# A decoder trunk on one core: VectorE waits for a GpSimd copy, and a group of weight loads waits for a transposed tile

## The reference

```python
for l in range(DEPTH):      # DEPTH = 2
    x = x + HALF_STEP * swiglu(rmsnorm(x, norm_ffn1[l]), w1_gate[l], w1_up[l], w1_down[l])
    ...                     # h = rmsnorm(x); differential attention and retention from h @ w_in
    x = x + mixed @ w_out[l]
    x = x + HALF_STEP * swiglu(rmsnorm(x, norm_ffn2[l]), w2_gate[l], w2_up[l], w2_down[l])
return rmsnorm(x, norm_final)
```

## Time and profile before

| | us |
|---|---|
| median of 3 runs | 958.66 (958.51 to 961.71) |
| profiled execution | 959.83 |
| its span in the trace | 957.9 |
| TensorE matmul busy | 945.5 (99% of the span) |
| VectorE busy | 556.7 (58%) |
| ScalarE busy | 460.5 (48%) |
| GpSimd busy | 189.2 (20%) |
| granted TensorE clock | 0.998 of full speed |

### The profile page before, as it was taken

How to read it: one execution, slowest core, us unless ns; L and a number is a source line. 1 busy time by engine, 2 the same in 40 slices (tenths; PEclk the granted TensorE clock), 3 DMA queues, 4 the chain that set the end, 5 groups by cost and what they waited for, 6 DMA issues and landing times.

```text
span 957.9 us, 12612 instructions
## 1 busy us (share of the span) xinstructions
PE 945.5 (99%) x4369; PEld 782.9 (82%) x4369; DVE 556.7 (58%) x632; ACT 460.5 (48%) x592; POOL 189.2 (20%) x239
## 2 busy tenths in 40 slices
PE   8999999999999999999999999999999999999997
PEld 6888888888888888888888888888888887888885
DVE  5545555666666565555656555556665756555554
ACT  7534444465563454444445444444657445444442
POOL 4344321000011322121033111110002024211110
PEclk9999999999999999999999999999999999999999
DMA  8897776634363886675647766663724657866641
GB/s 269 238 223 221 237 232 194 225 133 153 111 215 102 233 242 230 196 229 193 225 141 203 231 194 230 197 230 132 242 74 168 220 127 206 260 196 223 192 157 44
DMA packets 166339, 185.98 MB, mean 194 GB/s; under 512 B 49296, under 2 KB 139456, under 8 KB 166304
## 3 DMA queue, kind: packets, MB, share of 16 engines
q1 hardware_dynamic: 122368, 174.09, 54.2%
q10 hardware_dynamic: 43616, 10.52, 6.8%
q0 software_dynamic: 320, 0.92, 0.7%
HBM read 173.96 MB, written 1.05 MB: 183 GB/s over the span
## 4 chain that ended last, share of the span: by engine, by line
PE 93%; DMA 2%; ACT 2%; DVE 1%; POOL 1%; issue 0%; SPq 0%; POOLq 0%; DVEq 0%; ACTq 0%
PE gu L920 20%; PE gu L922 19%; PE gu L921 19%; PE acc L920 10%; PE acc L922 10%; PE acc L921 10%; DMA kT<-kT 2%; PE tp L1119 1%; DVE w_lo L628 1%; PE tp L938 1%; ACT w_hi L377 1%; PE acc L1130 1%; PE tp L1142 1%; DMA x<-in_x_dram 1%; PE gu L946 0%
## 5 line engine op out<-in xcount | busy, mean ns | idle before, releaser
L628 DVE TENSOR_TENSOR w_lo<-raw,w_hi 128x2048 fp32r<-128x2048 f32 (+1 forms) x164 | 375.1, 2292 | 153.1 <-ACT w_hi L377 152.7
L920 PE MATMUL gu<-w_hi,xT_hi 128*128 128x512 f32 x862 | 338.3, 392 | 0.2 <-DVE w_lo L628 0.2
L922 PE MATMUL gu<-w_hi,xT_lo 128*128 128x512 f32 x862 | 335.9, 390 | 0.0
L921 PE MATMUL gu<-w_lo,xT_hi 128*128 128x512 f32 x862 | 335.7, 389 | 0.0
L377 ACT ACTIVATE w_hi<-raw 128x2048 fp32r<-128x2048 f32 (+1 forms) x164 | 305.6, 1867 | 13.4 <-DMA raw<-in_w_in_dram 7.1
L920 PEld LDWEIGHTS gu<-w_hi,xT_hi 128*128 128x128 f32 x862 | 161.9, 188 | 33.9 <-DVE w_lo L628 0.6
L922 PEld LDWEIGHTS gu<-w_hi,xT_lo 128*128 128x128 f32 x862 | 161.8, 188 | 34.0
L921 PEld LDWEIGHTS gu<-w_lo,xT_hi 128*128 128x128 f32 x862 | 162.0, 188 | 32.5
L437 ACT ACTIVATE hid<-gu,st 128x256 f32<-128x256 f32 x86 | 40.6, 472 | 238.4 <-PE gu L922 200.6
L920 PE MATMUL acc<-w_hi,aT_hi 128*128 128x512 f32 x384 | 150.9, 393 | 1.6 <-DVE aT_lo L657 1.6
L922 PE MATMUL acc<-w_hi,aT_lo 128*128 128x512 f32 x384 | 149.8, 390 | 0.0
(11 more groups left out here) (157 smaller groups left out, 488.4 us busy)
## 6 DMA issues: line engine op xcount, KB each, us to landing
raw<-in_w_down_dram SPq DMA_DIRECT2D x88, 512.0 KB, 4.0
raw<-in_w_gate_dram SPq DMA_DIRECT2D x84, 512.0 KB, 3.9
raw<-in_w_up_dram SPq DMA_DIRECT2D x84, 512.0 KB, 4.8
raw<-in_w_in_dram SPq DMA_DIRECT2D x40, 512.0 KB, 4.6
raw<-in_w_out_dram SPq DMA_DIRECT2D x16, 512.0 KB, 4.1
raw<-in_w_in_dram SPq DMA_DIRECT2D x16, 256.0 KB, 2.8
raw<-in_w_gate_dram SPq DMA_DIRECT2D x8, 256.0 KB, 3.9
raw<-in_w_up_dram SPq DMA_DIRECT2D x8, 256.0 KB, 4.7
```

Of the source, the lines that this page charges most:

```text
L628: nc.vector.tensor_tensor(w_lo[:, pos % SLOTS, 0:n], raw[:, pos % RAW, 0:n], w_hi[:, pos % SLOTS, 0:n].bitcast(F32), ALU.subtract).then_in ...
L920: nc.tensor.matmul(out_, s_hi, m_hi, start=first, stop=False)
L921: nc.tensor.matmul(out_, s_hi, m_lo, start=False, stop=False)
L922: return nc.tensor.matmul(out_, s_lo, m_hi, start=False, stop=last)
```

## The change

Two waits are added, and nothing is removed.

On SyncE, in each FFN, a wait stands between the load of piece 4 and the loop that loads pieces 5 and on. It is for `halvesT_loaded[0]`, which a turn of tile 0 raises by 16, and the count is that of step 0's turn in this FFN. On VectorE, in step 0 of each FFN, a wait for GpSimd's parting of tile 0 stands between `hide` of tile 0 and what follows (split_lo of piece 3, or in the first FFN hide of tile 1).

```diff
@@ ffn on SyncE
                     load_gu(0, 0, 0)
                 load_gu(0, 2, 1)
                 load_down(0, 4, 0)
+                sp.wait_ge(halvesT_loaded[0], 16 * (STEPS - 1) * (2 * layer + (base > 0)) + 16)
                 with sp.Fori(0, LOOPED) as it:
                     for u in range(2):
                         load_gu(it, 5 + 3 * u, 2 * it + 2 + u)
@@ ffn on VectorE
                 def step(e, d, par, it, nxt, guard=True, banks=gu):
 
                     hide(e, 0, d - 1 if guard else None, banks)
+                    if not guard:
+                        dve.wait_ge(halves_done, d + 1)
                     nxt(0)
                     hide(e + 1, 1, d if guard else None, banks)
                     nxt(1)
```

## The result

The changed kernel takes 966.12 us (median of 6 runs, 965.44 to 966.99) against 961.05 for the kernel before (6 runs). The ratio is 1.0055, 95% interval 1.0039 to 1.0071: 5.3 us slower. The profiled executions differ by 6.9 us of span, 964.8 against 957.9. I use them for where the time went, not for how much it is. In the ratios of this document two executions of some 1365 us, at a granted clock of 0.65, are left out: one of c3 and one of the kernel before.

The account below looks back on a forecast made before the run. TensorE, busy 99% of the span, was taken as the bound. Lateness at piece 6 of 4.7, 2.0, 2.0 and 0.5 us, gains for tile 0 included, gave 958.66 + 9.2 = 967.9 us; own range 964 to 971, over the cases 957.9 to 971.

Parts of the forecast that it names:

- What can be gained: TensorE's waits for tile 0's low part, first and fourth FFN: at most 1.6 us from an earlier tile 0.
- VectorE's wait costs nothing: Step 0, second and fourth FFN: parting of tile 0 takes 0.61 us; the wait costs nothing by 0.4 us.
- Tile 0's turn is quick: Step 0's turn of tile 0 meets an empty queue and lands in 2.5 us, in time in all FFNs.
- Tile 1's turn goes behind the released loads: Step 0: tile 1's turn, issued amid four loads of pieces 5 and 6, lands 9.4 us after the first load.
- Two of the signs that I had named: In the changed kernel's profile, tile 1's step 0 turn lands in 8 us or more, just after the last load.
- A rule for it: DMA queues: the skill's rule of packets in turns would let a turn of 544 packets pass the loads.
- ScalarE's and VectorE's order carries it to piece 6: Step 2: piece 6's low part moves as much as tile 1's turned_hi: 5.0, 2.6, 3.3 and 0.9 us.
- The sum: TensorE's lateness at piece 6 over four FFNs, 4.7, 2.0, 2.0 and 0.5 us: +9.2 us.
- By turns or by position only: Rival, chance 0.20: tile 1's turn passes loads issued beside it, landing as with one piece ahead; -0.6 us, 958.1.
- Half way: Rival, chance 0.13: tile 1's turn takes 6.7 us, as in the second FFN before; +3.1 us, 961.8.

Follow-up runs that it names:

- c3: VectorE's wait alone, on the kernel before with each transposing turn replaced by two plain copies: 959.10 us, ratio 0.9985 to the kernel before.
- c6: Changed kernel with plain copies for the turns, plus a wait holding piece 6 for tile 1's rows: 962.10 us, ratio 1.0013 to the kernel before.
- c5: Changed kernel with plain copies, SyncE's wait moved between pieces 5 and 6 and made for tile 1's rows: 957.78 us, ratio 0.9977.
- c7: Changed kernel with plain copies, splits of pieces 5, 6 and 7 moved one place earlier on ScalarE and VectorE: 965.03 us, ratio 1.0049.
- c4: Changed kernel with plain copies, SyncE's wait before piece 5 made for tile 1's rows instead of tile 0's: 965.85 us, ratio 1.0056.
- c1: Changed kernel, both waits, with each transposing turn replaced by two plain copies: 966.34 us, ratio 1.0063 to the kernel before.
- c10: Changed kernel with plain copies, SyncE's wait for tile 0's rows moved from before piece 5 to between pieces 5 and 6: 962.33 us, ratio 1.0013.

## Why the prediction was right, point by point

**What can be gained.** Right in kind: the best two kernels with copies are 0.8 and 2.1 us below their base. In the profile both gain 1.8 us in the four stretches, 1.5 to 1.6 of it in the first FFN, where the base waited 1.1 us for aT_lo and 0.2 for w_lo. So the bound of 1.6 us, which counted only the waits for aT_lo, was a little too low.

**VectorE's wait costs nothing.** Right: piece 3 is reached without a wait in the second and fourth FFN, and c3 equals its base. With it the parting took 0.61 us.

**Tile 0's turn is quick.** Right: 2.5, 2.5, 2.4 and 3.1 us.

**Tile 1's turn goes behind the released loads.** Right in kind, and c6 and c5 show it by taking loads away. The size was off: I took 9.4 us from the first load to the landing. The trace has 7.1 in the first FFN (27.45 to 34.55), 8.5, 9.2 and 7.4. I had counted all four loads ahead of the turn. By the issue times one, two, three and one stood ahead of it (the second load of the fourth FFN followed within 0.04 us), and the landing, counted from the first load, follows that number. Two of the signs that I had named did not come: the turns took 6.7 to 7.9 us from their issue, not 8 or more, and they did not land just behind the last load. The DMA view of the first FFN shows where the turn's packets went; these are the stretches 27 to 30, 30 to 32 and 33 to 34 us (queue, packets, MB, share of the DMA engines):

```profile
q1 hardware_dynamic: 221, 0.23, 39.4%
...
q1 hardware_dynamic: 408, 0.40, 83.1%
q10 hardware_dynamic: 493, 0.13, 35.6%
...
q1 hardware_dynamic: 329, 0.32, 112.9%
q10 hardware_dynamic: 30, 0.00, 1.9%
```

The turn (q10, 544 packets) is issued at 27.85 and its packets come from 30.5 us on, when q1 had moved 402, not quite one load of 512. By 32 us 493 of them were through. The last 51 came among the loads until 34 us, and only with them does the turn land, at 34.55. The last load, issued at 29.29, landed at 37.3. From 30.5 to 32 us both queues moved: the turn's 493 packets and 227 of q1's (408 less the 181 before 30.5). In the second FFN, with two loads issued ahead of the turn, q1 had moved 894 packets before the turn's first one, and in the third, with three, 1301. So a turn starts when about as much has been moved as was issued before it; then it goes beside what is issued with it, and its tail sets the landing.

**A rule for it.** In these rows the order of issue sets when a turn's packets begin, and from there on both queues are served. The Trainium skill (DMA: Bandwidth & Descriptors, Queues, rings and completion order) has the DMA engine take packets in turns from the queues that have work. The trace agrees for the time from the first packet on, the tail above all. It does not for the start: the first packets came 2.7 us after the issue, where those of a turn without loads beside it (issued at 366.93 in the kernel before) came after 1.0 us. What holds the start back no run shows.

**ScalarE's and VectorE's order carries it to piece 6.** Right: GpSimd, ScalarE and VectorE show it as a chain, and c7 removed the waits for w_lo. I had put the whole wait at piece 6; TensorE met about half of it already at piece 5 (1.00 us there and 0.28 at piece 6 in the first FFN).

**The sum.** +9.2 us was forecast; the profiled executions have +7.8 in the four stretches, the runs 5.3. By FFN it was 4.7, 2.0, 2.0 and 0.5 against 2.9, 2.4, 2.8 and -0.3. With the landings as measured (7.1, 8.5, 9.2, 7.4) my sum would be 4.1, so the 9.4 was 5.1 us too much. The other terms were too small. From tile 0's parting to the first load it took 0.3 to 0.9 us more in each FFN than I had assumed, 1.9 us in all: from the turn's issue it is 2.8 to 3.4 us, not 2.5. And in the second FFN one issue of a turn took 2.16 us instead of 1.2, right on the chain; less a subtraction that was 0.2 us shorter, that is 0.8 us. In the third, VectorE's subtraction of piece 6 began while GpSimd was copying and took 2.84 us instead of 2.29, 0.6 us:

```profile
515.90 0.77 POOL L278 COPY qT<-kT 128x512 uint16<-128x512 uint16 x1
515.92 2.84 DVE L629 TENSOR_TENSOR w_lo<-raw,w_hi 128x2048 fp32r<-128x2048 f32 x1 [0.74 <-ACT w_hi L378]
```

This gives 7.4; the last 0.4 us is not accounted for. The runs' difference is 1.6 us less than that of the two spans; the execution profiled before (959.83) was itself 1.2 us under the median of all its runs, 961.05.

**Where luck helped.** The forecast of 967.9 us stands 1.8 us from the 966.12 measured, but the forecast of the change, 9.2 us, is 3.9 us from the 5.3 measured. The difference is the base: I added the sum to 958.66, the median of three runs, and with all six it is 961.05, 2.4 us more. On that base the same sum gives 970.3, still inside 964 to 971 but near its end. And the sum itself came as near as it did because one term too large (5.1 us) met several too small (3.3 us).

**The rivals.** "By turns or by position only" would have given -0.6 us; it is out, although position is part of the truth, and is why the landings were shorter than I took them. "Half way" took 6.7 us for the turn and +3.1 for the sum. The turn took 6.7, 7.8, 7.9 and 7.0 us, between that and the 7.9 to 8.7 that the forecast comes to from the turn's issue, and the 5.3 us of the runs are nearer to 3.1 than to 9.2, while the 7.8 of the profiles are nearer to the forecast. So the mechanism was the forecast's, and the size lay between the two cases.

## What to carry over

When a wait holds back prefetches until a small transfer has landed, look at what comes next behind that transfer. The held loads go out as a burst, and the next small transfer meets all of them. Place the hold so that no burst falls beside any transfer that the compute waits for: here, with plain copies, one wait between two pieces of weights, for the last of the small transfers, did what a wait ahead of both for the first could not. And a hold has an upper bound too: check when the held data is needed, counting from the release. Too late a release can cost more than the wait itself: in c4 a wait of 2.9 us was followed by 2.7 us lost to a lower clock.

## What the runs showed of the hardware

- A small DMA on another queue is not served ahead of loads that were issued before it. 64 KB took 2.0 us alone and 5.0 to 6.6 us when four 512 KB loads were issued within 1.6 us of it (c5 and c1); a 128 KB transposing DMA took 2.4 to 3.1 us alone and 6.7 to 7.9 us so.
- The order of issue counts: with a pair of loads begun 0.3 us ahead of it (and another pair 2.2 us behind) the small transfer took 6.0 us, with a pair begun 1.4 us behind it 2.1 us (c10). And a few packets can set the landing: 51 of 544 kept a turn open for over 2 us.
- After TensorE had stood idle for 2.88 us (c4) and 3.14 us (c7) its granted clock was 0.50 for 5.7 and about 3.4 us: 2.7 and 1.5 us lost beside the wait. By the mean clock of each execution, 4 of 6 of c4 and 10 of 12 of c7 were at 0.997 or less, and the fastest of both were at 0.998 and 0.999.
- GpSimd's copy took 2.49 us beside VectorE's subtraction of two float32 inputs and 0.61 without. The other way round VectorE's subtraction took up to 2.84 us instead of 2.29 when it started beside a running GpSimd copy.
